# Two early expert pairs of a mixture-of-experts layer in another order on TensorE and on the load queue

## The reference

```python
def swiglu(x, wg, wu, wd):
    return (jax.nn.silu(x @ wg) * (x @ wu)) @ wd

def moe_ffn(x, w_router, router_bias, w_gate, w_up, w_down, ws_gate, ws_up, ws_down):
    xf = x.reshape(B * S, D)                      # 256 tokens x 1024
    top_idx, top_w = route(xf, w_router, router_bias)
    y = routed_experts(xf, top_idx, top_w, w_gate, w_up, w_down) + swiglu(xf, ws_gate, ws_up, ws_down)
    return y.reshape(B, S, D)

def reference(x, mem, ...):
    for l in range(2):
        mix = hybrid_mixer(x, mem, ...)
        x = layer_norm(ALPHA * x + mix, ln1_g[l], ln1_b[l])
        ffn = moe_ffn(x, ...)
        x = layer_norm(ALPHA * x + ffn, ln2_g[l], ln2_b[l])
    return x
```

## Time and profile before

| what | us |
|---|---|
| median of 3 runs | 1187.55 (1187.35 to 1188.29) |
| the profiled execution | 1188.19 |
| its span in the trace | 1186.4 |
| PE busy | 1148.7 (97%) |
| DVE, ACT busy | 352.7, 255.3 |
| DMA | 456.49 MB, mean 385 GB/s |

### The profile page before, as it was taken

How to read it: one execution, slowest core, us unless ns; L and a number is a source line. 1 busy time by engine, 2 the same in 40 slices (tenths; PEclk the granted TensorE clock), 3 DMA queues, 4 the chain that set the end, 5 groups by cost and what they waited for, 6 DMA issues and landing times.

```text
span 1186.4 us, 15935 instructions
## 1 busy us (share of the span) xinstructions
PE 1148.7 (97%) x6752; PEld 523.0 (44%) x6752; DVE 352.7 (30%) x1053; ACT 255.3 (22%) x511; POOL 8.4 (1%) x20
## 2 busy tenths in 40 slices
PE   8999999999999999999999999999999999999995
PEld 7774633433343333333386655333343334333331
DVE  0424722222222222222333346232222222222224
ACT  1132421222122211111112323221222122112111
POOL 0000000000000000000000000000000000000001
PEclk9999999999999999999999999999999999999998
DMA  9982599999999999999998626999999999999995
GB/s 378 421 328 113 213 415 425 428 427 426 428 426 427 428 427 428 427 427 428 413 425 360 252 80 254 412 428 428 426 429 426 428 427 426 429 426 428 426 425 224
DMA packets 39952, 456.49 MB, mean 385 GB/s; under 512 B 4416, under 2 KB 4544, under 8 KB 8256
## 3 DMA queue, kind: packets, MB, share of 16 engines
q1 hardware_dynamic: 39872, 455.38, 91.5%
HBM read 452.22 MB, written 3.15 MB: 384 GB/s over the span
## 4 chain that ended last, share of the span: by engine, by line
PE 76%; DMA 21%; DVE 2%; issue 0%; ACT 0%; POOL 0%; POOLq 0%; DVEq 0%
PE bank L705 29%; DMA slots<-in_w_gu 20%; PE bank L725 14%; PE bank L926 5%; PE bank L854 5%; PE bank L607 4%; PE bank L634 4%; PE bank L863 2%; PE bank L1052 2%; PE bank L825 1%; PE bank L713 1%; PE bank L829 1%; PE bank L873 1%; PE bank L883 1%; PE bank L959 1%; PE bank L619 1%
## 5 line engine op out<-in xcount | busy, mean ns | idle before, releaser
L705 PE MATMUL bank<-slots,front 128*64 128x512 f32 x2048 | 456.0, 595 | 13.6 <-DMA slots<-in_w_gu 13.5
L705 PEld LDWEIGHTS bank<-slots,front 128*64 128x64 f32 x2048 | 139.9, 137 | 280.8 <-issue 249.4
L725 PE MATMUL bank<-slots,r 128*32 128x512 f32 x2016 | 229.9, 595 | 1.1 <-issue 1.1
L1403 DVE SCALAR_TENSOR_TENSOR yparts<-bank,small,yparts 128x512 fp32r<-128x512 f32 x128 | 96.0, 750 | 265.4 <-ACT yparts L1086 265.4
L1086 ACT ACTIVATE yparts<-bank,small 128x512 fp32r<-128x512 f32 x128 | 87.9, 687 | 239.8 <-PE bank L725 239.8
L1395 DVE TENSOR_TENSOR high<-high,bank 128x256 f32<-128x256 f32 x64 | 26.9, 421 | 354.5 <-ACT high L1113 326.7
L725 PEld LDWEIGHTS bank<-slots,r 128*32 128x32 f32 x2016 | 59.3, 109 | 137.2 <-issue 135.7
L1113 ACT ACTIVATE high<-bank 128x256 f32<-128x256 f32 x60 | 23.0, 384 | 413.1 <-PE bank L705 413.1
L1086 ACT ACTIVATE front<-bank 128x512 f32<-128x512 f32 (+1 forms) x161 | 84.5, 580 | 88.7 <-PE bank L825 28.2
L607 PEld LDWEIGHTS bank<-selr,xparts 128*128 128x128 f32 x512 | 64.3, 188 | 45.4 <-issue 45.4
L634 PE MATMUL bank<-yparts 64*128 64x512 f32 x512 | 79.4, 421 | 1.9 <-DVE yparts L1403 1.9
(11 more groups left out here) (123 smaller groups left out, 616.6 us busy)
## 6 DMA issues: line engine op xcount, KB each, us to landing
slots<-in_w_gu SPq DMA_DIRECT2D x116, 2048.0 KB, 30.8
slots<-in_w_dn SPq DMA_DIRECT2D x58, 2048.0 KB, 27.5
slots<-in_dense SPq DMA_DIRECT2D x28, 1024.0 KB, 14.8
slots<-in_w_gu SPq DMA_DIRECT2D x24, 1024.0 KB, 9.0
slots<-in_w_dn SPq DMA_DIRECT2D x10, 1024.0 KB, 37.4
slots<-in_first SPq DMA_DIRECT2D x3, 768.0 KB, 7.0
r<-in_pool_mat SPq DMA_DIRECT2D x2, 1024.0 KB, 25.9
sdn<-in_shared_dn SPq DMA_DIRECT2D x2, 1024.0 KB, 10.0
```

The lines of the kernel that those rows point to most:

```text
L705: m = pe.matmul(H[64 * a:64 * a + 64, :], cells[:, cell(B, k, j), a, :], GU[g][:, a, :, k, :], start=k == 0, stop=k == KD - 1)
L725: m = pe.matmul(Y[half][r0:r0 + 32, :], hT[:, kc * P + 64 * a + 32 * t:kc * P + 64 * a + 32 * t + 32], wd[:, a, kc, :], start=kc == 0, sto ...
L1403: dve.scalar_tensor_tensor(ysp[:, 1, half * 512:(half + 1) * 512], Y[half][:, :], wslot[:, b:b + 1], ysp[:, 0, half * 512:(half + 1) * 512 ...
```

## The change

Three things, in each of the two layers:

1. **Pair 2's last 2 MiB of gate/up weights come in two quarters of 1 MiB.** The first is sent for once the first four of the eight products of `sh1` are done (new semaphore `sgu_rd`), the second still behind `sh1`. Between them stands the first half of pair 3's down weights to `xs`. PE waits for the first of the quarters by a new semaphore, `third_in`.
2. **TensorE runs `gate_up` of pair 1 ahead of `down` of pair 0** (`first_two`). ACT and DVE have the orders that go with it. The two gathers of pair 1 move from behind its `gate_up` to behind `down` of pair 0 and `turn_h` of pair 1.
3. **SP issues the quarters of pairs 3 and 4 first, and then the down weights of pairs 3 and 4.** Before, pair 3's down weights stood between the quarters of pair 3 and those of pair 4.

The core of the diff; what DVE and ACT get is the order given in `first_two`:

```diff
                 if round_ is None:
+                    gates(base + 3, 3, 0)
+                    gates(base + 4, 4, 1)
+                    for q in (3, 4):
+                        sp.wait_ge(ps.y_full, 2 * (base + q - 2))
+                        load_dn(ps, l, q, q % 3)
+                pairs_of_pass(base, body, 5 if round_ is None else 3, ...)
...
-                sp.wait_ge(*full_at(l, "sh1"))
-                load_gu(main, l, 2, 2, (1,))
+                a, m, z = W_CHUNK, W_CHUNK + W_CHUNK // 2, 2 * W_CHUNK
+                sp.wait_ge(sgu_rd, l + 1)
+                sp.dma_start(slots[:, 2, a:m], w_gu[l * PAIRS + 2][:, a:m]).then_inc(third_in, 16)
                 sp.wait_ge(split_rd, 2 * l + 2)
                 sp.wait_ge(*full_at(l, "xTb3"))
                 sp.wait_ge(spill_out, 16 * l + 16)
                 sp.dma_start(xs[:]..., w_dn[l * PAIRS + SPLIT][:, 0:KF * D]).then_inc(ahead_in, 16)
+                sp.wait_ge(*full_at(l, "sh1"))
+                sp.dma_start(slots[:, 2, m:z], w_gu[l * PAIRS + 2][:, m:z]).then_inc(main.w_in[1][2], 16)
...
+                def first_two():
+                    pe.wait_ge(ps.sel_rd, first_block + 2)
+                    gate_up(base, 0, 0, 0, True)
+                    for i in range(2):
+                        gather(ps, i, Y[i])
+                    shared_turn(l, 1)
+                    turn_h(base)
+                    pe.wait_ge(ps.selT_sb, base + 1)
+                    turn_sel(ps, 1)
+                    gate_up(base + 1, 1, 1, 0, False)
+                    for n, q in ((base, 0), (base + 1, 1)):
+                        if q:
+                            turn_h(n)
+                            for i in range(2):
+                                pe.wait_ge(ps.lo_rd, 2 * n - 1 + i)
+                                gather(ps, 2 + i, Y[i])
+                            combine(ps, base, 0, 0, l)
+                            combine(ps, base, 0, 1, l)
+                        pe.wait_ge(ps.w_in[2][q], turn * USES[q] * 16 + 16)
+                        pe.wait_ge(ps.hT_sb, n + 1)
+                        for half in range(2):
+                            pe.wait_ge(ps.g_sb, first_fill + KD + 2 * q + half + 1)
+                            down(q, q, half)
+                    pe.wait_ge(ps.selT_sb, base + 2)
+                    turn_sel(ps, 2)
...
+                    elif t == 1:
+                        m.then_inc(sgu_rd, 1)
```

More of the change, by code:

```diff
@@ L321, in build @@
         quarter_rd = sem("quarter_rd")
+        sgu_rd = sem("sgu_rd")
+        third_in = sem("third_in")
         quarter_in = [[sem(f"quarter_in{i}_{h}") for h in range(2)] for i in range(3)]
@@ L479, in run, with gates @@
                         load_dn(ps, l, q, q)
-                def body(n, q, g, b, use, first, last):
+                def gates(n, q, g):
                     if round_ is None and q < 6:
@@ L493, in body @@
                         load_gu(ps, l, q, g, (1,))
+                def body(n, q, g, b, use, first, last):
+                    gates(n, q, g)
                     sp.wait_ge(ps.y_full, 2 * (n - 2))
                     load_dn(ps, l, q, g)
-                pairs_of_pass(base, body, 3, (lambda: load_count(sp, l)) if round_ is None else None)
+                if round_ is None:
+                    gates(base + 3, 3, 0)
[3 more added lines that the diff above has]
+                        load_dn(ps, l, q, q % 3)
+                pairs_of_pass(base, body, 5 if round_ is None else 3, (lambda: load_count(sp, l)) if round_ is None else None)
                 if round_ is None:
@@ L700, in gate_up @@
                         if k % 4 == 0:
+                            if round_ is None and q == 2 and k:
+                                pe.wait_ge(third_in, 16 * l + 16)
                             if round_ is None and 3 <= q < 6:
@@ L798, in last_two @@
                     down(q, g, 1)
-                pairs_of_pass(base, body, 0, (lambda: load_count(pe, l)) if round_ is None else None)
+                if round_ is None:
+                    first_two()
+                pairs_of_pass(base, body, 2 if round_ is None else 0, (lambda: load_count(pe, l)) if round_ is None else None)
                 if round_ is None:
@@ L1127, in hi @@
                             .then_inc(ps.hi_rd, 1)
-                pairs_of_pass(base, body, 0, (lambda: load_count(act, l)) if round_ is None else None)
+                if round_ is None:
+                    for q in range(2):
+                        act.wait_ge(ps.h_full, base + q + 1)
+                        act.activation(sg[:, 0, :], H[:, 0:F], ACT.Silu).then_inc(ps.silu_rd, 1)
+                        if q:
+                            hi(base, 0)
+                        for i in range(2):
+                            g_out(1, 2 * q + i, Y[i])
+                        if q == 0:
+                            shared_turned(l, 1)
+                    hi(base + 1, 1)
+                pairs_of_pass(base, body, 2 if round_ is None else 0, (lambda: load_count(act, l)) if round_ is None else None)
                 if round_ is None:
@@ L1405, in lo @@
                         .then_inc(ps.lo_rd, 1)
-                pairs_of_pass(base, body, 0, (lambda: load_count(dve, l)) if round_ is None else None)
+                if round_ is None:
+                    dve.wait_ge(ps.g_full, KD * (turn * BLOCKS + 1))
+                    build_sel(1)
+                    gated(base)
+                    turned(base)
+                    take_selT(base + 1, 1)
+                    gated(base + 1)
+                    dve.wait_ge(ps.selT_sb, base + 1)
+                    if l:
+                        dve.wait_ge(ps.lo_rd, 2 * base)
+                    lo(base, 0, 0)
+                    lo(base, 0, 1)
+                    turned(base + 1)
+                    dve.wait_ge(ps.selT_sb, base + 2)
+                    dve.wait_ge(ps.lo_rd, 2 * base + 2)
+                    lo(base + 1, 1, 0)
+                    lo(base + 1, 1, 1)
+                    take_selT(base + 2, 0)
+                pairs_of_pass(base, body, 2 if round_ is None else 0, (lambda: load_count(dve, l)) if round_ is None else None)
                 if round_ is None:
```

## The result

The changed kernel takes 1192.26 us (median of 5 runs, 1191.97 to 1194.55), the kernel before beside it 1187.55 us (5 runs). The ratio is 1.0042, with a 95% interval of 1.0031 to 1.0054: 4.7 us slower, where 1188.0 was forecast and 1190.2 was the upper end of the range. The profiled execution took 1192.19 us, with a span of 1190.4 us: 4.0 us more than the span before.

What follows compares the result with a forecast made beforehand. Each layer's end was set by when the load stream gets going for good, at pair 4's down weights, then by its bytes. Landings +0.14 and +0.34 us, +0.48 on the median 1187.55, gave 1188.0 us; range 1185.6 to 1190.2.

Steps and rivals of the forecast that it cites:

- The quarters of pairs 3 and 4: Loads on SP: pair 3's first quarter stays at 150.25 us; pair 4's are released 3.7 us earlier, by pair 1's `gate_up`.
- the gate: Issue of pair 4's down weights on SP, last break in each layer's load stream; forecast 0.67 us later, 175.18 and 760.05.
- 9.44 MB in 22.1 us at 427 GB/s: What the queue sends between 150.25 us and the issue of pair 4's down weights; all landed by 174.7 to 176.2 us.
- the sum: Change in landing time of pair 4's down weights, both layers together: +0.14 and +0.34, +0.48 us.
- The hole moves from 140 to 175 us: Almost nothing is sent from 134.5 to 145 us; filling this empties the queue before pair 4's down weights instead.
- The early issue: First 1 MiB quarter of pair 2, sent for at 140.6 us, 3.7 us ahead of the old issue at 144.26.
- The wait at the second gather: PE waits 0.77 us for DVE to read Y[1] before pair 1's second gather, near 169 us.
- The landing on an empty queue: Pair 4's down weights, 2 MiB, land 7.87 us after issue, the mean of six; bounds 7.2 and 8.7 us.
- The marks: Signs expected in the changed profile: issue times, PE's idle near 169 us, an empty queue, PE meeting loads at 407 us.
- the three signs of being wrong: Pair 4's down weights issued well before 174 us, queue still sending then, or no 427 GB/s behind 200 us.
- The rival that ended on the slow side: PE's wait before pair 1's second gather is twice the reckoned one, with the dearest landing: 1191.2 us, chance 0.08.
- The rival of the filled hole: The 1 MiB sent early in each layer reaches the end, two times 2.46 us: 1182.6 us, chance 0.07.

Runs made afterwards that it cites:

- the three pairs with quarters: Changed kernel, wait moved back, half combine between gathers; added: `gate_up` of pair 2 before `down` of pair 1, pair 5's quarters before pair 4's down weights: 1188.33 us.

## Why the prediction was wrong

**The step that failed** is in "The quarters of pairs 3 and 4": the first quarter of pair 3 is released by `gate_up` of pair 0, "which doesn't move: 150.25 us". It moved by 1.93 us, since the first line of `first_two` is a wait that had stood behind this product. The line is in the diff that the prediction had before it; its working lists what the moved products wait for, but not this wait, which stands ahead of a product that keeps its place. In the trace PE goes on in the order of its program (`gate_up`, which doesn't read `selr`, starts 0.05 us after that is written), so the wait held all that stands behind it: `gate_up` of pair 0, the quarters that it releases, the other products and the gate. Moving the line back gives 3.35 us, and the wait alone makes the old kernel slower by 7.3 (a fall of the clock included).

**The second one** is in the same part: "9.44 MB in 22.1 us at 427 GB/s". The price of starting on an empty queue was known. The working adds it once behind those 22.1 us, but takes nothing from the gain for it, and the sum pays it only at the gate. With the MiB sent early the queue runs down already at 150 us, so it is paid there too: in the kernel with the wait moved back the stretch of 150 to 154 us runs at 246 and 315 GB/s. "The hole moves from 140 to 175 us" was half of it; it moves to 150 first. With the new order this hardly shows in the time. The quarters alone cost 2.9 us, of which the split may have a part, and the three pairs with quarters missed their expectation, with thin stretches in the trace; that these made them miss is likely, not shown.

**What held.** The view of the whole: the end of a layer follows the gate's landing (+1.97 and +2.27 us against +1.99 and +2.41; less closely in the other kernels, as said above), and the stretch behind 200 us runs at 427 GB/s. The early issue (140.6 forecast, 140.23 found, with a layer that began 0.4 us earlier). The wait at the second gather (0.77 forecast, 0.69 found). The gate counted from `gate_up` of pair 0: 176.78 - 149.80 = 26.98 us; before 174.51 less 148.29, where `gate_up` then started, 26.22; so +0.76 for 0.67. The landing on an empty queue (7.87 forecast, 7.7 and 7.8 found). Without the first step's error the forecast would have stood 0.9 us off, by the run with the wait moved back.

**The marks.** "`gate_up` of pair 1 at 157.5" was 159.03; "the issue near 175.2 and 760.1 us" was 176.78 and 763.64. "PE should meet the loads at 407 us plus or minus 1" was 395.87: PE and the loads are late by nearly the same, but the meeting comes 11 us earlier, and why it does wasn't followed up. "An empty queue of one to two microseconds ahead of" the gate was less in layer 0: from 174.50 to 176.78 us the rate is 356 GB/s, 0.4 us of sending lost, since most of the hole had gone to 150 us. Of the three signs of being wrong none came clearly (the gate was late and not early, the rate was down to 194 GB/s in the last 0.38 us ahead of it, and behind 200 us it was 427): all three look at the gate and behind it, and the mistake lay ahead of it. The rival that ended on the slow side had the right sign and almost the price (1191.2 us) with the wrong place: it put the growing wait in front of the second gather, where it was smaller than reckoned. The rival of the filled hole is refuted: the first part of the change alone, which starts the MiB in the hole, made the kernel slower.

## What to carry to other kernels

When a sequence is rewritten by hand, list its waits as well as its work: for each wait that has changed place, name the first instruction behind it that doesn't need it, and what that instruction releases. In this kernel an early transfer wasn't worth its bytes where the queue emptied sooner for it; look at the next issue, what releases that, and how much is still queued then. Find the last place where the stream of loads starts anew, and cost each change by what it does there.

## What the runs showed of the hardware

- A transfer added to a thin queue can pay for itself: with 1 MiB more per layer the profiled kernel with the quarters carried 16.27 MB of use in 45 us instead of 16.12 (layer 1: 16.27 instead of 15.90).
- The DMA share hides a thin queue. In 162 to 167 us of the kernel with quarters alone the engines count as 0.96 busy and move 305 GB/s; in the changed kernel from 200 to 300 us a share of 1.01 goes with 427. The rates show it, the shares hardly do. Why fewer bytes go with nearly the same busy share isn't settled.
- After 1.77 us without work on PE the granted clock was 0.50 for about three microseconds in one layer of one kernel (`gate_up` 8.78 us instead of 7.06), and stayed full after the same idle time in the other layer and in both layers of the changed kernel. In the twelve profiles there are 16 pauses of 1.3 us or more between 40 and 1180 us. After five of them (1.77, 2.05, 2.10, 2.55 and 2.70 us) the products were slowed; after the other eleven, of 1.36 to 2.27 us, they weren't. So in this range the length of the pause alone doesn't tell.
